# A hybrid decoder block: twenty expert rows dotted on TensorE, five late rows moved ahead of the value stage

## What is computed

```python
def peer_ffn(xn, wq, sub_keys, u_tab, v_tab):
    q = (xn @ wq).reshape(B, S, PEER_HEADS, 2, PEER_HALF)
    s = jnp.einsum('bshpd,hpnd->bshpn', q, sub_keys)
    top_v, top_i = lax.top_k(s, PEER_TOPK)                     # 16 of 128, twice
    cand_v, cand_i = lax.top_k(<16 x 16 sums>, PEER_TOPK)
    experts = i1 * PEER_NKEYS + i2                             # 16 of 16384 a head
    gates = jax.nn.softmax(cand_v, axis=-1)
    act = jax.nn.gelu(jnp.einsum('td,tkd->tk', xb, u_tab[eb])) # the dots
    return jnp.einsum('tk,tkd->td', gb * act, v_tab[eb])       # the values
```

## Time and profile before

| | us |
|---|---|
| median of 3 runs | 2682.72 (2682.69 to 2687.92) |
| the profiled execution | 2683.64 |
| its span | 2681.6 |

### The profile page before, as it was taken

How to read it: one execution, slowest core, us unless ns; L and a number is a source line. 1 busy time by engine, 2 the same in 40 slices (tenths; PEclk the granted TensorE clock), 3 DMA queues, 4 the chain that set the end, 5 groups by cost and what they waited for, 6 DMA issues and landing times.

```text
span 2681.6 us, 33701 instructions
## 1 busy us (share of the span) xinstructions
PE 2163.6 (81%) x12145; PEld 1874.2 (70%) x12145; DVE 2062.4 (77%) x2612; ACT 1265.2 (47%) x2004; POOL 692.9 (26%) x343
## 2 busy tenths in 40 slices
PE   8999999999999899999999600003419999999997
PEld 7997789999988788889889500003317777777775
DVE  7885556566654855664468999999998999999999
ACT  4464544444444443454355301775835444444444
POOL 1000000000000100010001487886862343343341
PEclk9999999999999999999999855556759999999999
DMA  7453565555465455564457898999988999999997
GB/s 235 134 159 119 179 195 165 158 157 157 156 214 187 157 187 188 174 207 154 135 179 289 319 390 333 388 411 400 406 332 330 421 422 421 421 421 421 421 421 311
DMA packets 273965, 728.95 MB, mean 272 GB/s; under 512 B 21192, under 2 KB 164768, under 8 KB 215856
## 3 DMA queue, kind: packets, MB, share of 16 engines
q1 hardware_dynamic: 226432, 385.65, 41.3%
q0 software_dynamic: 46912, 340.81, 31.5%
q10 hardware_dynamic: 496, 0.84, 0.1%
HBM read 725.14 MB, written 2.10 MB: 271 GB/s over the span
## 4 chain that ended last, share of the span: by engine, by line
PE 57%; DVE 23%; DMA 16%; issue 2%; ACT 2%; POOL 0%; DVEq 0%; ACTq 0%; POOLq 0%
PE bank L419 19%; PE bank L441 18%; DVE b_u_ring L2218 14%; PE bank L468 10%; DMA b_v_raw<-in_peer_v 7%; DMA b_late_row<-in_peer_v,b_idx_all 4%; DMA b_late_row<-in_peer_u,b_idx_all 4%; PE bank L1729 3%; PE bank L1741 2%; PE bank L1517 1%; DVE b_hN L2292 1%; DVE b_late_row L2285 1%; PE bank L1401 1%; DVE b_v_lo L2268 1%; ACT b_v_hi L1289 1%
## 5 line engine op out<-in xcount | busy, mean ns | idle before, releaser
L405 DVE TENSOR_TENSOR b_w_both<-b_raw,b_w_both 128x1024 fp32r<-128x1024 f32 x464 | 566.4, 1239 | 443.5 <-ACT b_w_both L400 442.4
L400 ACT ACTIVATE b_w_both<-b_raw 128x1024 fp32r<-128x1024 f32 x464 | 484.0, 1057 | 551.0 <-PE bank L419 214.1
L836 POOL DMA_INDIRECT b_u_ring<-in_peer_u,b_idx_all x192 | 411.3, 2142 | 154.3 <-DVE b_dots L2218 81.2
L2218 DVE CUSTOM_DVE_ANT_0 b_u_ring<-b_u_ring,b_xnN 128x2048 f32<-128x2048 f32 x192 | 434.7, 2275 | 0.0
L1729 PE MATMUL bank<-b_v_hi,b_e_parts 128*128 128x512 f32 x1536 | 381.2, 397 | 33.7 <-DVE b_e_parts L2273 22.0
L1289 ACT ACTIVATE b_v_hi<-b_v_raw 128x1024 fp32r<-128x1024 f32 x256 | 257.1, 1052 | 299.7 <-DVE b_v_lo L2268 150.1
L1729 PEld LDWEIGHTS bank<-b_v_hi,b_e_parts 128*128 128x128 f32 x1536 | 282.9, 189 | 125.1 <-DVE b_e_parts L2273 34.8
L419 PE MATMUL bank<-b_w_both,b_act_both 128*128 128x512 f32 x1536 | 355.0, 391 | 2.5 <-ACT b_w_both L400 2.5
L419 PEld LDWEIGHTS bank<-b_w_both,b_act_both 128*128 128x128 f32 x1536 | 288.5, 189 | 62.7 <-ACT b_w_both L400 3.0
L441 PE MATMUL bank<-b_act_both,b_w_both 128*128 128x256 f32 x2688 | 328.4, 284 | 0.0
L441 PEld LDWEIGHTS bank<-b_act_both,b_w_both 128*128 128x128 f32 x2688 | 324.2, 192 | 1.6 <-issue 1.3
(11 more groups left out here) (315 smaller groups left out, 2418.3 us busy)
## 6 DMA issues: line engine op xcount, KB each, us to landing
b_v_raw<-in_peer_v SPq DMA_DIRECT2D x128, 1024.0 KB, 11.2
b_raw<-in_w_in SPq DMA_DIRECT2D x208, 512.0 KB, 4.4
b_raw<-in_w_proj_dsa SPq DMA_DIRECT2D x32, 512.0 KB, 4.4
b_raw<-in_w_proj_gla SPq DMA_DIRECT2D x32, 512.0 KB, 4.2
b_raw<-in_w_xk SPq DMA_DIRECT2D x32, 512.0 KB, 3.3
b_raw<-in_w_out SPq DMA_DIRECT2D x32, 512.0 KB, 3.3
b_raw<-in_w_xv SPq DMA_DIRECT2D x32, 512.0 KB, 4.6
b_raw<-in_w_xq SPq DMA_DIRECT2D x32, 512.0 KB, 3.3
```

The lines of the kernel that those rows point to most:

```text
L400: act.activation(w_hi[:, q], raw[:, UQ * c + q], ACT.Copy).then_inc(w_high, 1)
L405: dve.tensor_tensor(w_lo[:, q], raw[:, UQ * c + q], w_hi[:, q].bitcast(F32), ALU.subtract).then_inc(w_split, 1)
L836: pool.indirect_dma_start(u_ring[:, s], None, u_rows, bass.IndirectOffsetOnAxis(ap=idx_all[:, at:at + 1], axis=0)).then_inc(u_landed[s], 16)
L2218: dve.tensor_tensor_reduce(u, u, xnN[:, g // PEER_H], 1.0, 0.0, ALU.mult, ALU.add, dots[:, g * PTOP + k:g * PTOP + k + 1]).then_inc(sem("d ...
```

## The change

- `TURNED_ROWS`: 20 of the 128 rows of groups 0 to 7 are not dotted by VectorE: rows 3, 7, 11 and 15 of groups 1 to 3, rows 7 and 15 of groups 4 to 6, rows 3 and 11 of group 7. For each of them TensorE turns the gathered 128 x 2048 row in four quads of four 128 x 128 blocks into two banks (`turn_quad`), ScalarE copies each quad (`copy_row`), and TensorE multiplies the turned blocks with the turned tokens `xn_turned` into a 128 x 128 product (`dot_quad`). VectorE takes its diagonal (`add_diagonal`) where the next turned row comes in its order; for the last one after row 127. The slot of such a row is free when its last quad is turned (`row_used`).
- The tokens are turned once, ahead of group 1, into `xn_turned`; ScalarE copies them.
- In groups 4 to 7 ScalarE does its 9 (at last 5) marks in two parts with a `copy_row` behind each; the exponents come behind both. In groups 1 to 3 the exponents come behind four `copy_row`s.
- The seed of banks 4 to 7 comes on TensorE behind the last turned row and its diagonal instead of ahead of all; banks 4 to 7 are used by the turned rows before that.
- `ROWS_AMID`: VectorE does late steps 0 to 4 behind the marks of octets 3, 5, 9, 11 and 13. The other 123 late rows are spread over the value tiles. Late rows 0 and 1 are gathered at once after the last dot, 2 and 3 behind the clearing of `hN` (and the steps that free their places), 4 and 5 after eight octets. There is a sixth place for late rows, in the later place of `v_hi`; ScalarE's second value tile waits for four late steps.
- `distances` and some `oct_cols` lie elsewhere; octet columns 6 and on wait for the 32 units.

```diff
+FIRST_PLACES = (0, 5, 0, 5, 2, 0, 1)
+ROWS_AMID = {3: 0, 5: 1, 9: 2, 11: 3, 13: 4}
+TURNED_ROWS = tuple(g * PTOP + k for g, ks in ((1, (3, 7, 11, 15)), (2, (3, 7, 11, 15)), (3, (3, 7, 11, 15)), (4, (7, 15)),
+                                               (5, (7, 15)), (6, (7, 15)), (7, (3, 11))) for k in ks)
+QUADS = 4
+BLOCKS_TURNED, BLOCKS_COPIED, ROWS_TURNED = 24, 16, 8
...
+    def row_used(eng, n):
+
+        if n in TURNED_ROWS:
+            eng.wait_ge(sem("turned_in"), BLOCKS_TURNED + quad(TURNED_ROWS.index(n), QUADS))
+        else:
+            eng.wait_ge(sem("dotted"), dotted_at(n))
...
-        return [m for m in range(LATE_ROWS) if LATE_FROM + LATE_SPAN * m // LATE_ROWS == n]
+        amid = len(ROWS_AMID)
+        return [m for m in range(amid, LATE_ROWS) if LATE_FROM + LATE_SPAN * (m - amid) // (LATE_ROWS - amid) == n]
...
-        late_rows(0, 1)
+        late_rows(0, 2)
         pool.wait_ge(sem("seeded"), 1)
         pool.memset(hN[0:SHARED, 1], 0.0).then_inc(sem("late_cleared"), 1)
+        late_rows(2, 4)
+        pool.wait_ge(sem("unit_spread"), HALF + 8)
+        late_rows(4, 6)
         pool.wait_ge(sem("rows_by_vector"), OCTETS)
         pool.wait_ge(sem("gate_exped"), GROUPS)
-        late_rows(1, 2)
-        pool.wait_ge(sem("unit_spread"), UNITS)
-        late_rows(2, LATE_ROWS)
+        late_rows(6, LATE_ROWS)
...
+        def copy_row(r):
+
+            for q in range(QUADS):
+                act.wait_ge(sem("turned_in"), BLOCKS_TURNED + quad(r, q) + 1)
+                wait(act, sem("rows_turned"), ROWS_TURNED + quad(r, q) - 2 - QUADS + 1)
+                act.activation(row_turned[:, q % 2].rearrange("p k t -> p (k t)"), bank[4 + q % 2], ACT.Copy
+                               ).then_inc(sem("copied_in"), 1)
...
-            if g >= MARKED_FROM:
-                for u in range(made, min(made + MARKED_A_GROUP, HALF)):
+            rows = [r for r, n in enumerate(TURNED_ROWS) if n // PTOP == g]
+            marked = min(MARKED_A_GROUP, HALF - made) if g >= MARKED_FROM else 0
+            for i, r in enumerate(rows):
+                for u in range(made, made + marked * (i + 1) // len(rows) - marked * i // len(rows)):
                     mark_unit(u)
                     made = u + 1
+                copy_row(r)
             for r in routes_in(g):
                 gate_exp(r)
...
+        def turn_quad(i, src):
+
+            wait(pe, sem("copied_in"), BLOCKS_COPIED + i - 1)
+            for b in range(KT // QUADS):
+                kt = i % QUADS * (KT // QUADS) + b
+                mm = pe.transpose(bank[4 + i % 2][:, b * P:(b + 1) * P], src[:, kt * P:(kt + 1) * P], ident)
+            mm.then_inc(sem("turned_in"), 1)
+
+        def dot_quad(r, q):
+
+            pe.wait_ge(sem("copied_in"), BLOCKS_COPIED + quad(r, q) + 1)
+            for b in range(KT // QUADS):
+                kt = q * (KT // QUADS) + b
+                mm = pe.matmul(bank[6 + r % 2][:, 0:P], row_turned[:, q % 2, b], xn_turned[:, kt], start=(kt == 0), stop=(kt == KT - 1))
+            mm.then_inc(sem("rows_turned"), 1)
+
+        def dot_turned_row(r):
+
+            n = TURNED_ROWS[r]
+            pe.wait_ge(*row_landed(n))
+            for q in range(QUADS):
+                turn_quad(quad(r, q), u_ring[:, row_slot[n]])
+                if q == 1 and r >= 2:
+                    pe.wait_ge(sem("dotted"), dotted_at(TURNED_ROWS[r - 2]))
+                if q > 0:
+                    dot_quad(r, q - 1)
+            dot_quad(r, QUADS - 1)
+
         pe.wait_ge(sem("sims_ready"), PEER_H)
-        seed(range(4, 8)).then_inc(sem("seeded"), 1)
+        pe.wait_ge(sem("rows_normed"), 1)
+        for q in range(QUADS):
+            turn_quad(q, xnN[:, 0])
+        before_tables = sum(n < MARKED_FROM * PTOP for n in TURNED_ROWS)
+        for r in range(before_tables):
+            dot_turned_row(r)
         pe.wait_ge(sem("routed"), PEER_H)
         turn_tables(0, (isel_all[:, 0], isel_all[:, 1]), 0, 0)
+        for r in range(before_tables, len(TURNED_ROWS)):
+            dot_turned_row(r)
+        pe.wait_ge(sem("dotted"), dotted_at(TURNED_ROWS[-1]))
+        seed(range(4, 8)).then_inc(sem("seeded"), 1)
...
+        def add_diagonal(r):
+
+            dve.wait_ge(sem("rows_turned"), ROWS_TURNED + QUADS * (r + 1))
+            dve.tensor_tensor_reduce(diagonal, bank[6 + r % 2][:, 0:P], ident, 1.0, 0.0, ALU.mult, ALU.add,
+                                     dots[:, TURNED_ROWS[r]:TURNED_ROWS[r] + 1]).then_inc(sem("dotted"), 1)
...
             if o == 1:
                 normalize(EARLY, GROUPS)
+            if o in ROWS_AMID:
+                late_step(ROWS_AMID[o])
```

More of the change, by code:

```diff
@@ L645, in row_before, with dotted_at, quad @@
         return same[-1] if same else None
+    dot_order = []
+    for n in range(EARLY * PTOP):
+        if n not in TURNED_ROWS:
+            dot_order.append(n)
+        elif n != TURNED_ROWS[0]:
+            dot_order.append(TURNED_ROWS[TURNED_ROWS.index(n) - 1])
+        if n == PEER_H * PTOP - 1:
+            dot_order.append(TURNED_ROWS[-1])
+    def dotted_at(n):
+        return dot_order.index(n) + 1
+    def quad(r, q):
+        return QUADS + QUADS * r + q
+    def row_used(eng, n):
[3 more added lines that the diff above has]
+            eng.wait_ge(sem("dotted"), dotted_at(n))
     def places(count, first, grow):
@@ L657, in hybrid_block, with late_row_landed, late_before @@
     tile_place, tile_back = places(NKEYS, len(v_raw), {})
-    row_place, row_back = places(LATE_ROWS, 3, ROWS_GROW)
+    row_place, held = list(FIRST_PLACES), 3
+    for m in range(len(FIRST_PLACES), LATE_ROWS):
+        held += m in ROWS_GROW
+        row_place.append(held - 1 if m in ROWS_GROW else row_place[m - held])
+    def late_row_landed(m):
+        if row_place[m] < LATE_PLACES:
+            return landed(late_landed, row_place, m)
+        s = SLOT_OF_PLACE[row_place[m]]
+        return u_landed[s], 16 * (row_slot.count(s) + row_place[:m + 1].count(row_place[m]))
+    def late_before(m):
+        same = [n for n in range(m) if row_place[n] == row_place[m]]
+        return same[-1] if same else None
     def landed(sems, place, n):
@@ L714, in hybrid_block @@
     v_landed = [sem(f"v_landed{s}") for s in range(len(v_raw))]
-    late_landed = [sem(f"late_landed{s}") for s in range(len(late_row))]
+    late_landed = [sem(f"late_landed{s}") for s in range(LATE_PLACES)]
     w_in = a["w_in"][0]
@@ L833, in gather_rows @@
                 if before is not None:
-                    pool.wait_ge(sem("dotted"), before + 1)
+                    row_used(pool, before)
                 s = row_slot[at]
@@ L846, in late_rows @@
                     pool.wait_ge(sem("e_split"), ROWS_GROW[m])
-                elif m >= 3:
-                    pool.wait_ge(sem("late_used"), m - row_back[m] + 1)
-                where, count = landed(late_landed, row_place, m)
+                elif late_before(m) is not None:
+                    pool.wait_ge(sem("late_used"), late_before(m) + 1)
+                where, count = late_row_landed(m)
                 pool.indirect_dma_start(late_row[row_place[m]], None, (u_rows, a["peer_v"][0])[kind],
@@ L1275, in expert_gelu @@
         def expert_gelu(lo, hi):
-            act.wait_ge(sem("dotted"), hi)
+            act.wait_ge(sem("dotted"), max(dotted_at(n) for n in range(lo, hi)))
             return act.activation(w_all[:, lo:hi], dots[:, lo:hi], ACT.Gelu_apprx_tanh)
@@ L2213, in dot_row @@
         def dot_row(g, k):
+            n = g * PTOP + k
+            if n in TURNED_ROWS:
+                if n != TURNED_ROWS[0]:
+                    add_diagonal(TURNED_ROWS.index(n) - 1)
+                return
             if g == PEER_H and k == 0:
                 dve.wait_ge(sem("rows_packed"), 3)
-            dve.wait_ge(*row_landed(g * PTOP + k))
+            dve.wait_ge(*row_landed(n))
             u = u_ring[:, row_slot[g * PTOP + k]]
@@ L2282, in late_step @@
                 dve.wait_ge(sem("weights_ready"), g - EARLY + 3)
-            dve.wait_ge(*landed(late_landed, row_place, m))
+            dve.wait_ge(*late_row_landed(m))
             if kind == 0:
```

23 lines of the change are left out of this document (18 added, 5 removed).

## The result

| | before | after |
|---|---|---|
| median of the compared runs, us | 2684.50 (10 runs, 2682.69 to 2691.32) | 2689.98 (10 runs, 2685.24 to 2699.53) |
| ratio | | 1.0020 (95% interval 1.0011 to 1.0029) |
| span of the profiled execution, us | 2681.6 | 2687.2 |

The change makes the kernel 0.2% slower, 5.4 us (3.0 to 7.8). The forecast was 2679, 4.5 us faster, so its sign is wrong; the time lies in the range of 2658 to 2697, near the rival of ScalarE's queue (2688).

The account below looks back on a forecast made before the run. The prediction took VectorE's dots as the bound, DMA close behind, then DMA after the octets. Moving dots to TensorE (-1.9 us) and five late rows amid the octets (-2.6) gave -4.5: 2679 us, range 2658 to 2697.

Parts of the forecast that it names:

- rival of ScalarE's queue: Groups 4 to 7: copy_rows of 7.2 us between marks, 2688 us in all; decides from a copy_row of 6.6; chance 0.18.
- Groups 1 to 3: Twelve turned rows there leave DMA as the bound; group 4 begins at 1660 instead of 1666, 6 us earlier.
- the wait in route(6): Group 3: VectorE waits until 1647.6 for ScalarE's exponent of group 5, queued behind the copy_row of row (3, 15).
- Groups 4 to 7: ScalarE becomes the bound with eight copy_rows of 6.3 us; the stage takes 170 us, not 165.9, 4 us lost.
- The clock: TensorE, idle before each turned row, runs 4 us cold at half clock, then full; a row is done after 8.3 us.
- rival of half clock throughout: Turned rows: TensorE never reaches full clock, a row takes 11.8 us, the whole 2710 us; chance 0.09.
- Groups 8 to 11: Only VectorE's dots, so the stage stays at 166.8 us; the later seed of banks 4 to 7 costs nothing.
- The octets: No room for five late steps between VectorE's and TensorE's alternating work; the stage becomes 9.8 us longer.
- part 2: Five late rows done amid the octets: +9.8 us there, -12.4 us afterwards, net -2.6 us (+2 to -4).
- The value stage: DMA-bound stretch after the octets: 247 transfers to go instead of 252, at 2.49 us each, so -12.4 us.
- Part 1: Dots of twenty turned rows on TensorE in groups 1 to 7: -6 and +4.1 us, sum -1.9 us.
- Faster: Sign of the whole change: measurably faster than the kernel before, chance 0.43, against 0.27 same and 0.30 slower.

Follow-up runs that it names:

- e5: Changed kernel with ScalarE taking group 5's exponent ahead of the copy_row of row (3, 15); query products' end to group 4 146.0 us instead of 149.8.
- e4: Changed kernel with a mark's distances in one instruction a table instead of four, so marks aren't the reference's; 2682.64 us, ratio 0.9988 to the kernel before.
- e6: Changed kernel with one mark moved into each copy_row of groups 4 to 7; executed once, that stage took 160.2 us.
- e9: Changed kernel with value-stage late rows respread, none at tiles 12, 24, 36, one each at 122 to 126; 2689.16 us, ratio 1.0015 to the kernel before.
- e10: Changed kernel with the edits of e5, e6 and e9 together; 2670.62 us, ratio 0.9950 to the kernel before.
- e2: Changed kernel without turned rows, the five late rows amid the octets kept; ratio 1.0013 (1.0004 to 1.0022) to the kernel before.
- the seven: Kernels with late rows amid the octets and the changed kernel's own value-stage tail, that kernel included; last dot to end 686.8 us on the mean.
- the three without part 2: The kernel before and two follow-up kernels with turned rows but its octets and value stage; last dot to end 684.0 us on the mean.

## Why the prediction was right or wrong

**Groups 1 to 3: right in kind, 1.2 us short.** The gain was to be 6 us and is 4.8; the wait in route(6) is there (4.68 us), and e5 shows that the wait was the limit. GpSimd's wait before group 4 is as long as before (15.0 us against 14.0).

**Groups 4 to 7: right.** 170 forecast, 170.3 measured. The diagonals take 0.285 + 0.085 us (0.35 taken). The copy_rows are 5.2 to 6.7 us, 49.6 for all eight, where the sum took 50. The slot of row (7, 3) is free 145.3 us after G4, where it took 147. ScalarE is the bound (e4, e6). The rival of ScalarE's queue put copy_row at 7.2 us and is wrong in that; its point of 6.6 was not reached on the mean (6.2). So the total came near that rival's 2688 for another reason.

**The clock: right in kind, the 4 us not.** In groups 4 to 7 seven of the eight rows start at half clock, after 10.7 to 12.9 us without work, and full clock comes 3.9 to 10.3 us later, waits for ScalarE included, and not 4. That cost little: there the first two quads lie turned before ScalarE comes, so its copies wait only for what follows. In groups 1 to 3, with 1.4 to 5.2 us without work ahead of a row, two of twelve rows are at full clock from the start, and the mean is 0.80. The rival of half clock throughout fell.

The argument for that rival was that no row of before shows transposes alone at full clock after an idle stretch. There is one. At 8.09 us TensorE starts, out of 8.09 us without work, on 32 transposes and nothing else; four of them take 1.06 us at first, and six 0.82 at the end.

```profile
8.76 1.06 PE L624 MATMUL bank<-b_consts,b_xN 128*128 128x128 f32 x4
13.40 0.82 PE L624 MATMUL bank<-b_consts,b_xN 128*128 128x128 f32 x6
```

The Trainium skill, "TensorE: Matmul & The Clock Gate", "Part 4: PE-mode transpose", says that full speed doesn't engage for transposes, and that they don't count as busy in the same way. The traces don't agree, by these two lines and by the last transposes of the turned rows, 0.60 us for four against 1.06 earlier.

**Groups 8 to 11: right,** 167.0 in both; TensorE's late seed costs nothing there.

**The octets: right,** +9.6 in the pair, +10.2 to +11.7 in the other kernels with part 2. Not all of it is the late steps. GpSimd's second gather and the clearing of `hN` behind it now both lie beside the first marks: four of them take 3.23 us instead of 1.99, and 1.11 where GpSimd does nothing. And TensorE has a mean clock of 0.73 instead of 0.85.

**The value stage: this step failed.** It took five transfers less as 12.4 us less at the end of the kernel. U-end fell by 8.1. The DMA part holds: the windows have 265 GB/s over 35.7 us amid the octets, 9.5 MB, against 161 over 26.1, 4.2 MB; those are the five transfers, and from U to the last take of a tile it is 623.0 us instead of 634.8, 11.8 less. But the step took the end of the DMA-bound stretch for the end of the kernel. The last late row is now at tile 125 and not at 126, so the last three tiles come 2.8 us apart, and TensorE needs 2.72 + 1.81 = 4.5 for each. It falls behind, and 3.7 us of the gain come back in the tail, a term that the sum doesn't have. e9 shows it: with a row at tile 126 the tail is 22.7 us, not 25.7, as in e10.

That makes part 2 +1.5 us in the pair of profiles (+9.6 - 8.1) where -2.6 was forecast. On the mean of the kernels it is +2.8, in e2's timing +3.5 (1.1 to 5.9). The +2.8 of the seven against the three without part 2 are +10.7 for the octets (9.8 forecast), -11.0 from U to the last take (-12.4) and +3.1 in the tail (0 in the forecast): the tail is more than half of the 5.4 us that the forecast is off there. The pair was a lucky one: after's last tile comes 658.8 us after D, 660.0 to 663.3 in the other kernels with part 2, 661.0 before. What decides these 4 us isn't settled.

**The sum.** Part 1: -1.9 forecast, -0.1 in the pair (-4.8 + 4.7). Part 2: -2.6 forecast, +1.5 in the pair, +2.8 on the mean. So -4.5 became +1.4 to +2.7; timed it is +5.4 (3.0 to 7.8). That comes close to the nearer end of the interval. What is missing would lie before E, where the sum has nothing. The profiles scatter there from 1511.3 to 1516.8 with the same instructions, and in the pair the 4.2 us are TensorE's clock, which was at half for longer at three places. The two kernels without turned rows have 1511.5 and 1511.4, the eleven with them 1514.8 on the mean; but e9 has 1511.3 with all turned rows, so it isn't a fixed cost of theirs. Whether such programs lose the clock more often on the mean stays open.

**The chances.** "Faster" had 0.43, and the rival on the slower side had a place that the runs don't bear out. No rival had the tail, though the rows had both numbers: TensorE busy 596 of 630 us is 4.7 us a tile, more than the 2.49 of a tile without a late row.

## What to carry to other kernels

A stretch that is bound by transfers ends with the engine that consumes them: where transfers are taken out of it, check the spacing of the last ones against the consumer's time for each, and keep the filler work up to the last tile. When work goes to an engine that already has some, count the waits inside the new step as that engine's time, and put its own old work into them; here the order alone was worth 10 us in a stretch of 170, and the move was only seen to pay (0.5 to 0.6%) with it. A short item that somebody waits for (0.7 us of exponents) goes ahead of a long step on the same queue.
